# Sampled tokens' attention as a pipeline over batches, and keys and values with stationary weights, in a decoder step on one NeuronCore

## Chip, cores and metric

The kernel is one program on one core of a Trainium2 chip. The metric is its device time in microseconds (us). All matrix work runs on TensorE (PE), element work on VectorE (DVE), ScalarE (ACT) and GpSimd (POOL); SyncE (SP) and POOL issue the DMAs.

## What is computed

One step of a two-layer decoder for 256 prompt tokens and 8 batches of 8 sampled tokens (320 columns together). Layer 0 is a feed-forward block, a convolution module and another feed-forward block; its result gives the keys and values that layer 1 attends to. Cut to what the change touches:

```python
rows = (rmsnorm(x, g_kv) @ w_kv).reshape(B, T, 6, N_KV, HEAD_DIM)   # k_cmp v_cmp k_slc v_slc k_win v_win
kc = compress(k_cmp rows); vc = compress(v_cmp rows)                # gelu(blocks @ w1 + b) @ w2 + b2
p_c = masked_softmax(q kc * scale - slope * dist)                   # compressed branch
imp = (p_c summed over the group) @ overlap                         # importance of 33 blocks of 64 rows
idx = top_k(score(imp), 16)                                         # selected branch reads these blocks
o = g0 * attend(kc, vc) + g1 * attend(selected blocks) + g2 * attend(window of 512)
```

For a sampled batch the keys are 2048 paged rows in 16 pages (selected branch, all rows scored and the blocks not chosen pushed to -1e30), 512 window rows, 127 compressed rows and the 8 new rows.

## The kernel before

**Activations** are kept transposed, channels on partitions and 320 tokens on the free axis. A float32 product is three products of fp32r halves (`product`, L562 to L564). Weights stream in slabs of 1 MB: SP loads one, ACT splits off the high half (`split`, L1045), DVE the low half (`low`, L1406), PE multiplies it. `ffn`, `slabs` and `down` are loops over slabs.

**Keys and values** (phase `kv`, 6 slabs of 256 columns, one for each kind of row). `kv` in the PE program makes the tokens the stationary operand and streams the 256 columns of weights: for each of 3 token tiles (128, 128, 64) and 8 k-steps one `product`, 72 matmuls for a slab. DVE's `kv_rows` (L1701, L1703) scales them into `rows` and `rowsS`. Then 12 transposes (L791) turn the rows of the selected and the window keys into `kT`, and ACT copies them (L1259).

**The prompt's compression** comes after the query phase `q` and the gates. POOL has written the rows to `out_kv_prompt`; SP reads them back in blocks of 16 rows (L448) with the first layer's weights (L449). The class `Compression` then works 16 steps: ACT relays a piece (L1131), PE turns it (L673), ACT copies it out (L1137), PE multiplies it (`first_layer`, L813), and in the end the second layer. The prompt's attention starts behind it (L826).

**The cached compression** (8 batches) uses the same class inside layer 0, with gathers on POOL (L504) for half a batch at a time.

**Attention of the sampled tokens.** In a loop over the batches PE's `batch_scores` works in this order: transposes of the last batch's probabilities (`turn_probs`, L922) mixed with the transposes of this batch's keys (`turn_keys`, L943, 10 groups of 4), the compressed scores, the importance (L968, L974), five chunks of 512 scores (`chunk`, L937), and then `batch_values` of the batch before (L986, 92 small products). DVE adds the bias to each chunk (L1878), picks the blocks, finds the window's maximum (L1902), adds the drop to 2048 columns (L1907), finds the maximum of 2112 (L1909); ACT takes the exponentials (L1358, L1361); DVE scales by the sums (L1916, L1917); only then can the probabilities be turned. There is one score area `S`. Pages of keys go to `kpg`, issued by SP, pages of values to `vpg`, issued by POOL (`load_pages`, L329 to L331: a register load, an address and a DMA for each page); SP also loads each batch's window rows (1 MB, L464) into one of two slots of `W`. The engines are in order: what waits on an engine holds up all behind it.

Of the kernel before, what the change touches and what calls it, by code (L numbers as in the profile page):

```python
# [14 lines left out]
P = 128  # L15
# [42 lines left out]
S_SEL, S_NEW, S_WIN, S_WNEW, S_CMP = 0, PAST, PAST + TS, PAST + TS + WIN, PAST + 2 * TS + WIN  # L58
S_COLS = S_CMP + P
CREDIT = 2  # L60


def host_constants():
# [39 lines left out]
        ("sel_bias", sel_bias), ("cmp_bias_p", cmp_bias_p.reshape(P, -1)),  # L103
    ]
# [55 lines left out]
def program(nc, ins, outs, where):  # L160
    with ExitStack() as ctx:
# [43 lines left out]
        cslot = sb("cslot", P, CS, dt=I32)  # L205
# [23 lines left out]
        def slab_views(*shape):  # L229
# [29 lines left out]
        RTp = area(HF, 0, 2, 2, 66)  # L259
# [6 lines left out]
        STGp = [area(GF, u * 4096, 8, 512) for u in range(2)]  # L266
        qT = area(GF, 8192, KT, T)
        w1p = area(GF, 8192 + KT * T, 2, 16, P)
        PT = area(GF, 8192 + KT * T, 23 * P)
        qbd = area(GF, 8192 + KT * T + 23 * P, 2, P)  # L270
        selb = area(HF, 0, PAST)
        KTb = area(SF, 0, 2, PAST)
        S = area(SF, 4096, S_COLS)
        KTw = area(SF, 4096 + S_COLS, 2, WIN)
        osb = tmp[:, 0, 0:P]
        ips = tmp[:, 1, 0:P]
        wst = [W[:, u, :].rearrange("p (r c) -> p r c", r=WR) for u in range(2)]
# [20 lines left out]
            conv_step ln_step hist_out cen_ready idx_ready slot_ready rt_turned rt_ready rl_ready vnew_ready  # L298
            z_ready gelu_ready kv_ready kv_out conv_turned conv_rows stored kT_turned kT_out prow_loaded
# [3 lines left out]
            s_scores s_biased c_max c_exp c_scaled imp_sum imp_sumout imp_ready s_max s_exp s_scaled pt_turned  # L303
            pt_out o_ready o_copied o_turned o_out qbd_ready selb_loaded ptrow_loaded y_turned y_out pool_step""".split()
# [4 lines left out]
        gathered = [sem("gathered0"), sem("gathered1")]  # L309
        half_used = [sem("half_used0"), sem("half_used1")]  # L310
        K_loaded, V_loaded, K_used, V_used = map(sem, ("K_loaded", "V_loaded", "K_used", "V_used"))
        V_last_loaded = sem("V_last_loaded")
        win_loaded = [sem("win_loaded0"), sem("win_loaded1")]
        win_used = [sem("win_used0"), sem("win_used1")]
# [4 lines left out]
        OUTS_KV = 2 * (FT + KT) + KT + 4 + 6  # L319
        OUTS_DOWN10 = OUTS_KV + FT + KT  # L320

        cache = ins["cache_kv"]

        def load_pages(eng, b, c, page, used, count, loaded):

            eng.wait_ge(used, count)
            eng.sem_inc(m["passed"], 1)
            for k in range(NPAGE):
                n = eng.value_load(ptrow[0:1, bass.ds(b * NPAGE + k, 1)], min_val=0, max_val=NPOOL - 1)  # L329
                src = cache[bass.ds(n, 1), :, c, :, :].rearrange("a t g d -> t (a g d)")  # L330
                eng.dma_start(page[:, k, :], src).then_inc(loaded, 16)  # L331


        def sp_program(sp):
# [96 lines left out]
            slabs("kv", wide(ins["w_kv"].rearrange("(k p) n -> p k n", p=P)))  # L431
# [12 lines left out]
            sp.wait_ge(m["kv_stored"], 16)  # L444
            sp.wait_ge(m["evac_done"], OUTS_DOWN10 + CREDIT)
            for u in range(2):
                src = outs[2][0].rearrange("(n s) c g d -> n s (c g d)", s=CS)[:, 8 * u:8 * u + 8, 0:512]
                sp.dma_start(STGp[u][0:NCP], src).then_inc(m["prow_loaded"], 16)  # L448
                sp.dma_start(w1p[:, u, :, :], ins["w_cmp1"][u].rearrange("(j s) d h -> (s d) j h", s=2)) \  # L449
                  .then_inc(m["w1p_loaded"], 16)  # L450
# [17 lines left out]
            with sp.Fori(0, NB // 2 - 1) as i:  # L468
                for u in range(2):
                    load_keys(i, u + 1)  # L470
# [17 lines left out]
        def pool_program(pool):  # L488
# [54 lines left out]
            with pool.Fori(1, NB - 1) as b:  # L543
                load_pages(pool, b, 3, vpg, V_used, b + 1, V_loaded)
# [1457 lines left out]
```

## Time and profile before

| | |
|---|---|
| median of 3 runs | 1906.74 us (1906.7 to 1912.01) |
| the profiled execution: time, span | 1903.35 us, 1901.5 us |
| busy: PE, DVE, ACT, POOL | 1729.9, 1178.8, 720.4, 217.7 us |
| chain that ended last | PE 83%, DVE 8%, ACT 3%, issue 3% |
| mean granted clock of TensorE | 0.934 |

The profiled execution spent 1.85 us outside its span. A busy PE counts matmuls whose ends are modelled, so intervals between starts are the better measure. PEclk is the granted clock of TensorE: 1.00 is 2.4 GHz, 0.50 is 1.2 GHz. An "idle before" is put down to the releaser that came last.

### The profile page before, as it was taken

What the parts mean: (1) busy time and instruction counts of PE and PEld (TensorE: products, weight loads), DVE (VectorE), ACT (ScalarE), POOL (GpSimd) and SP (SyncE); (2) the same over time, 40 slices, a digit from 0 to 9 for tenths busy, and PEclk for the clock granted to TensorE, in tenths of its full rate; (3) what the DMA queues carried; (4) which work ended last, traced back from release to release, by engine and by line L of the source; (5) the groups of instructions that cost most, each with busy time, mean ns of one, the idle gap of its engine ahead of it and who ended that gap; (6) DMA issues with size and microseconds to landing.
All of it is one profiled execution on the core that took longest, in us unless ns stands there. A gap on an engine that the chain in (4) does not pass through costs nothing.

```text
span 1901.5 us, 35340 instructions
## 1 busy us (share of the span) xinstructions
PE 1729.9 (91%) x12409; PEld 1599.1 (84%) x12409; DVE 1178.8 (62%) x2082; ACT 720.4 (38%) x1090; POOL 217.7 (11%) x294
## 2 busy tenths in 40 slices
PE   6999999999999699999999999988857666999996
PEld 5999998788787699999999999976635545899995
DVE  6665565788886776655456655315566665766644
ACT  4332343555555443333233333235323424333321
POOL 0000021344453000000010000011003321000000
PEclk9999999899999899999999999957878888999998
DMA  5556575344445545545455545631035556455452
GB/s 145 155 152 170 146 203 148 105 116 124 120 126 209 172 124 142 153 137 155 128 159 148 154 129 156 128 97 41 7 117 191 180 176 183 125 155 144 130 152 66
DMA packets 368061, 264.72 MB, mean 139 GB/s; under 512 B 30880, under 2 KB 350867, under 8 KB 366689
## 3 DMA queue, kind: packets, MB, share of 16 engines
q1 hardware_dynamic: 350640, 202.77, 38.5%
q0 software_dynamic: 17344, 60.89, 10.2%
q8 instruction: 53, 0.87, 0.2%
q14 instruction: 24, 0.19, 0.0%
HBM read 259.95 MB, written 12.64 MB: 143 GB/s over the span
## 4 chain that ended last, share of the span: by engine, by line
PE 83%; DVE 8%; ACT 3%; issue 3%; SPq 1%; DMA 1%; DVEq 0%; POOL 0%; ACTq 0%
PE PSA L562 23%; PE PSA L564 22%; PE PSA L563 22%; PE PSA L673 3%; PE PSA L943 2%; PE PSA L937 2%; PE PSA L922 1%; PE PSA L870 1%; DVE small L1909 1%; PE PSA L813 1%; DVE S_f L1907 1%; DVE S_f32r L1406 1%; PE PSA L704 1%; PE PSA L703 1%; DVE S_f L1878 1%
## 5 line engine op out<-in xcount | busy, mean ns | idle before, releaser
L562 PE MATMUL PSA<-H_f32r,S_f32r 128*128 128x320 f32 (+1 forms) x1984 | 656.8, 331 | 25.3 <-DVE H_f32r L1542 24.3
L564 PE MATMUL PSA<-H_f32r,S_f32r 128*128 128x320 f32 (+1 forms) x1984 | 642.3, 324 | 0.0
L563 PE MATMUL PSA<-H_f32r,S_f32r 128*128 128x320 f32 x1728 | 539.9, 312 | 0.0
L1406 DVE TENSOR_TENSOR S_f32r<-W,S_f32r 128x2048 fp32r<-128x2048 f32 (+1 forms) x178 | 365.0, 2051 | 120.3 <-ACT S_f32r L1045 112.7
L562 PEld LDWEIGHTS PSA<-H_f32r,S_f32r 128*128 128x128 f32 x1984 | 379.3, 191 | 36.4 <-issue 23.5
L1045 ACT ACTIVATE S_f32r<-W 128x2048 fp32r<-128x2048 f32 (+1 forms) x178 | 305.2, 1714 | 272.7 <-PE PSA L564 260.3
L564 PEld LDWEIGHTS PSA<-H_f32r,S_f32r 128*128 128x128 f32 x1984 | 378.8, 191 | 11.9
L563 PEld LDWEIGHTS PSA<-H_f32r,S_f32r 128*128 128x128 f32 x1728 | 329.8, 191 | 0.5 <-issue 0.2
L563 PE MATMUL PSA<-G_f32r,S_f32r 128*128 128x320 f32 (+1 forms) x960 | 320.2, 334 | 0.0
L562 PE MATMUL PSA<-G_f32r,S_f32r 128*128 128x320 f32 x704 | 217.7, 309 | 1.2 <-DVE S_f32r L1406 1.2
L564 PE MATMUL PSA<-G_f32r,S_f32r 128*128 128x320 f32 x704 | 217.6, 309 | 0.0
L1078 ACT ACTIVATE tmp<-tmp 128x320 f32<-128x320 f32 x96 | 45.4, 472 | 443.5 <-DVE tmp L1476 443.5
L563 PEld LDWEIGHTS PSA<-G_f32r,S_f32r 128*128 128x128 f32 x960 | 182.0, 190 | 5.9
L1476 DVE TENSOR_TENSOR tmp<-PSA,stat 128x320 f32<-128x320 f32 x96 | 47.2, 491 | 181.9 <-PE PSA L564 181.0
L1649 DVE SCALAR_TENSOR_TENSOR H_f<-G_f,wdw,H_f 128x256 f32<-128x256 f32 x480 | 152.3, 378 | 0.0
L504 POOL DMA_INDIRECT G_f<-in_cache_kv,cslot x128 | 128.2, 1002 | 48.9 <-issue 35.8
L562 PEld LDWEIGHTS PSA<-G_f32r,S_f32r 128*128 128x128 f32 x704 | 132.2, 188 | 1.4 <-issue 1.4
L564 PEld LDWEIGHTS PSA<-G_f32r,S_f32r 128*128 128x128 f32 x704 | 132.2, 188 | 0.0
L331 POOL DMA_DIRECT2D G_f<-in_cache_kv x112 | 62.4, 557 | 504.8 <-issue 504.8
L1137 ACT ACTIVATE H_f32r<-PSA 128x512 fp32r<-128x512 f32 x128 | 76.7, 599 | 114.0 <-PE PSA L673 113.4
L1639 DVE TENSOR_TENSOR G_f32r<-PSA,H_f32r 128x512 fp32r<-128x512 f32 x128 | 88.3, 690 | 47.4 <-ACT H_f32r L1137 47.4
L673 PEld LDWEIGHTS PSA<-const,W 128*128 128x128 f32 (+1 forms) x576 | 73.9, 153 | 25.8 <-issue 4.7
(259 smaller groups left out, 1890.7 us busy)
## 6 DMA issues: line engine op xcount, KB each, us to landing
W<-in_w_ff_in SPq DMA_DIRECT2D x176, 512.0 KB, 5.0
W<-in_w_ff_out SPq DMA_DIRECT2D x64, 704.0 KB, 4.5
G_f<-in_cache_kv SPq DMA_DIRECT2D x144, 128.0 KB, 2.4
G_f<-in_cache_kv POOLq DMA_DIRECT2D x112, 128.0 KB, 3.0
W<-in_w_pw SPq DMA_DIRECT2D x16, 512.0 KB, 5.1
W<-in_state_kv_win SPq DMA_DIRECT2D x8, 1024.0 KB, 6.7
out_win_sample<-in_state_kv_win POOLq DMA_DIRECT2D x1, 8064.0 KB, 9.7
W<-in_w_kv SPq DMA_DIRECT2D x6, 1024.0 KB, 5.0
```

The lines of the kernel that those rows point to most:

```text
L331: eng.dma_start(page[:, k, :], src).then_inc(loaded, 16)
L504: pool.indirect_dma_start(out=STG[u][:, s, :], out_offset=None, in_=pairs, in_offset=bass.IndirectOffsetOnAxis(ap=cslot[:, 8 * u + s:8 * u ...
L562: pe.matmul(out, w[0], x[0], start=start, stop=False)
L563: pe.matmul(out, w[0], x[1], start=False, stop=False)
L564: return pe.matmul(out, w[1], x[0], start=False, stop=stop)
L673: tr = pe.transpose(PS[5 + c][:, g * n:g * n + n], RL[0:n, c, g * P:g * P + P], ident[0:n, 0:n])
L1045: act.activation(flat_slab[u][HI][:, 0:ph.cols], flat_slab[u][RAW][:, 0:ph.cols], ACT.Copy) \
L1137: act.activation(self.RT[:, j % 2, c, 0:4 * n], PS[5 + c][:, 0:4 * n], ACT.Copy) \
L1406: dve.tensor_tensor(lo, raw, hi, ALU.subtract).then_inc(m["lo_ready"], 1)
L1476: dve.tensor_tensor(tmp[:, u, :], PS[2 * u + gate][:, 0:T], stat[:, 2, :], ALU.mult) \
L1639: dve.tensor_tensor(RTs[1][:, j % 2, c, 0:4 * P], PS[5 + c][:, 0:4 * P], RTs[0][:, j % 2, c, 0:4 * P], ALU.subtract).then_inc(m["rt_ready" ...
L1649: dve.scalar_tensor_tensor(o, x(b * TAPS_AT_ONCE + (a + 1)), wdw[:, bass.ds(b * (TAPS_AT_ONCE * KT) + (a * KT + KT + k), 1)], o, ALU.mult, ...
```

## The change

Three things change at once.

1. **Keys and values.** The weights become the stationary operand: `keys_and_values` does 8 k-steps by 2 halves of one `product` with 320 columns, 48 matmuls for a slab, and leaves keys and values transposed. `turn_rows` turns each of the 6 results into rows (6 transposes), in the middle of the next slab. For the first two kinds DVE copies the transposed rows into `blocksT` (8 copies each), and the prompt's first and second layer of the compression run right behind the last slab and between the first two slabs of `up10`. Its relays, transposes and the way through DRAM are gone.
2. **Attention of the sampled tokens.** Two score areas take turns. `chunk` adds the drop itself, by two more matmuls of 512 columns (`dropT` by `block_keys`) on the four chunks of the selected branch; DVE adds bias and finds the minimum of the negated scores in one instruction (`tensor_tensor_reduce`); the sums and gates are applied to the output (`combine`), not to the probabilities. The keys of the next batch are turned between the chunks of this one, and the values of the batch before come behind the chunks. Pages are loaded in quads with their own semaphores. The window rows move from SP's queue to POOL's and have three slots.
3. **Cached compression.** The gathers are released and awaited by pairs; the loop is written out, and the copy of the indices is gone.

```diff
+        def load_quad(eng, b, i, c, page, loaded):
+            _, numbers = nc.values_load_multi_w_load_instructions(
+                ptrow[0:1, b * NPAGE + QUAD * i:b * NPAGE + QUAD * i + QUAD], engines=[eng.engine], ...
+            for k, n in enumerate(numbers, QUAD * i):
+                eng.dma_start(page[:, k, :], src).then_inc(loaded[i], 16)
...
+                if c == 1:
+                    sp.wait_ge(m["evac_done"], OUTS_DOWN01 + CREDIT)
+                    for w in range(2):
+                        sp.dma_start(w1p[:, w, :, :], ins["w_cmp1"][w]...).then_inc(m["w1p_loaded"], 16)
...
-            with pool.Fori(1, NB - 1) as b:
-                load_pages(pool, b, 3, vpg, V_used, b + 1, V_loaded)
+            load_window(1)
+            for b in range(1, NB):
+                if b > 2:
+                    pool.wait_ge(win_used, b - 2)
+                    load_window(b)
+                for i in range(QUADS):
+                    if b < NB - 1:
+                        pool.wait_ge(V_used, QUADS * (b - 1) + i + 1)
+                        load_quad(pool, b, i, 3, vpg, V_loaded)
...
+            def turn_rows(c):
+                pe.wait_ge(m["evac_done"], OUTS_DOWN01 + CREDIT + c + 1)
+                for t, (at, n) in enumerate(TOK_TILES):
+                    for h in range(2):
+                        mm = pe.transpose(out, src[:, h, at:at + n], ident)
+            def keys_and_values(first):
+                for c in range(ph.n):
+                    for k in range(KT):
+                        if c and k == KT // 2:
+                            turn_rows(c - 1)
+                        for h in range(2):
+                            mm = product(PS[2 * u + h][:, 0:T], [W256[u][p][:, k, h * P:h * P + P] for p in (HI, LO)],
+                                         [x[:, k, :] for x in hR], k == 0, k == KT - 1)
...
+            keys_and_values(rows_in(row_mean))
+            prompt_first_layer(0)
+            prompt_first_layer(1)
+            turn_rows(PH["kv"].n - 1)
+            ffn("10", mean=False, between=prompt_second_layer)
...
-            prompt.batch(NB)
-            prompt.end(NB)
...
+            def chunk(b, c):
+                for q in range(2):
+                    mm = pe.matmul(bank[half, :], qbd[:, u, q, half], keys, start=True, stop=c == QUADS)
+                if c < QUADS:
+                    pe.wait_ge(m["drop_out"], b + 1)
+                    for q in range(2):
+                        mm = pe.matmul(bank[half, :], dropT[blocks, half], block_keys[blocks, :], start=False, stop=True)
...
+            def values(b):
+                value(AT_WIN, 21, TS, rowsS[:, 5, :], first=True)
+                for c in range(WR):
+                    mm = value(AT_WIN, NPAGE + c, P, wst[b][:, c, 256:512], last=c == WR - 1)
+                mm.then_inc(win_used, 1)
+                value(AT_CMP, 22, P, vc[:, b, :], first=True, last=True)
+                value(AT_SEL, 20, TS, rowsS[:, 3, :], first=True)
+                for k in range(NPAGE):
+                    mm = value(AT_SEL, k, P, page[:, k, :], last=k == NPAGE - 1)
+                    if k > QUAD and k % QUAD == 1:
+                        mm.then_inc(V_used, 1)
+            def turn_out(b):
+                pe.wait_ge(m["o_combined"], b + 1)
+                pe.matmul(PS[7][0:HD, 256:384], osb, ident, start=True, stop=True).then_inc(V_used, 1)
...
+            for b in range(NB):
+                chunk(b, 0)
+                chunk(b, 1)
+                small_scores(b + 1); turn_quad(b + 1, 0)
+                chunk(b, 2)
+                turn_quad(b + 1, 1)
+                chunk(b, 3)
+                importance_sum(b + 1)
+                chunk(b, 4)
+                importance(b + 1)
+                values(b - 1)
+                turn_quad(b + 1, 2)
+                turn_probs(b, 0); turn_probs(b, 1)
+                turn_out(b - 1)
+                turn_quad(b + 1, 3)
+                turn_probs(b, 2); turn_probs(b, 3)
+                turn_drop(b + 1); turn_quad(b + 1, 4)
+                turn_probs(b, 4); turn_probs(b, 5)
```

(In the last piece the conditions `if more` and `if b` are left out, and some calls share a line.)

The order on POOL, in the loop over the batches of the sampled tokens: one register load, then an address and a DMA for a page. Before, for each page:

```order
L329 ISA [waits V_used]
L329 TENSOR_LOAD ptrow
L329 ISA x2
L331 ISA
L331 DMA G_f<-in_cache_kv 128x256
L329 ISA
L329 TENSOR_LOAD ptrow
L329 ISA x2
L331 ISA
L331 DMA G_f<-in_cache_kv 128x256
```

Now, at the last quad of batch 2's values and the window rows of batch 3 (L349 is the page's DMA, L546 the window's):

```order
L344 TENSOR_LOAD ptrow [waits V_used]
L349 ISA
L349 DMA G_f<-in_cache_kv 128x256
L349 ISA
L349 DMA G_f<-in_cache_kv 128x256
L349 ISA
L349 DMA G_f<-in_cache_kv 128x256
L349 ISA
L349 DMA G_f<-in_cache_kv 128x256
L546 DMA W<-in_state_kv_win 128x2048 [waits win_used]
L344 TENSOR_LOAD ptrow [waits V_used]
```

The register load stands once for four pages, and the window's DMA stands behind the last quad of the batch before.

The order on PE from the turned output to the window keys, one batch's turn (L1093, L1094 `turn_out`; L1005 keys; L1062 probabilities; L1026 the drop):

```order
L1093 MATMUL PSA<-const,tmp 64x128 [waits o_combined]
L1094 MATMUL PSA<-const,tmp 64x128
L1005 MATMUL PSA<-const,G_f 128x128 [waits kt_out0,K_loaded3]
L1005 MATMUL PSA<-const,G_f 128x128 x3
L1005 MATMUL PSA<-const,G_f 128x128 [waits kt_out1]
L1005 MATMUL PSA<-const,G_f 128x128 x3
L1062 MATMUL PSA<-const,S_f 128x128 [waits pt_out,s_exp]
L1062 MATMUL PSA<-const,S_f 128x128 x3
L1062 MATMUL PSA<-const,S_f 128x128 [waits pt_out,s_exp]
L1062 MATMUL PSA<-const,S_f 128x128 x3
L1026 MATMUL PSA<-const,G_f 128x128 [waits drop_ready]
L1005 MATMUL PSA<-const,W 128x128 [waits kt_out1,win_loaded0]
```

Seventeen transposes stand between the output's turn, which frees the last quad of value pages, and the first use of the next batch's window rows.

## Rows read from the trace of the kernel before

**Rows 1.** The page's chain that ended last, by engine

```profile
PE 83%; DVE 8%; ACT 3%; issue 3%; SPq 1%; DMA 1%; DVEq 0%; POOL 0%; ACTq 0%
```

**Rows 2.** Windows: length, busy of PE, PEld, DVE, ACT, POOL; PEclk, DMA share, GB/s

```profile
1235.00:1266.00 31.00, 28.98 (x150) 24.46 (x150) 0.70 (x3) 14.40 (x39) 0.00 (x0) 0.50 0.04 10
1365.80:1607.10 241.30, 162.72 (x2272) 114.49 (x2272) 149.21 (x335) 82.93 (x164) 53.72 (x96) 0.85 0.53 162
```

**Rows 3.** Timeline of DVE (start, length): two `kv` slabs, then two of `up10`

```profile
911.34 0.88 DVE L1701 TENSOR_SCALAR rows<-PSA,rtok 128x256 f32 x2 [1.79 <-PE PSA L564]
919.84 0.88 DVE L1701 TENSOR_SCALAR rows<-PSA,rtok 128x256 f32 x2 [4.38 <-PE PSA L564]
...
969.42 0.49 DVE L1476 TENSOR_TENSOR tmp<-PSA,stat 128x320 f32<-128x320 f32 x1 [5.33 <-PE PSA L564]
...
976.46 0.49 DVE L1476 TENSOR_TENSOR tmp<-PSA,stat 128x320 f32<-128x320 f32 x1 [1.91 <-PE PSA L564]
```

**Rows 4.** Timeline of PE between `kv` and `up10`

```profile
953.34 0.28 PE L564 MATMUL PSA<-S_f32r,H_f32r 128*64 128x256 f32 x1
954.97 0.44 PE L791 MATMUL PSA<-const,rows 128*128 128x128 f32 x2 [1.35 <-DVE rowsS L1703]
...
959.42 0.61 PE L562 MATMUL PSA<-H_f32r,S_f32r 128*128 128x320 f32 x1 [2.10 <-DVE H_f32r L1542]
```

**Rows 5.** Chain that ended last (start, length): the prompt's compression and what follows

```profile
1239.24 1.04 PE PSA L813 x4
...
1266.06 7.04 PE PSA L826 x64
```

**Rows 6.** Timeline of DVE: the sampled tokens' gates

```profile
1236.49 0.35 DVE L1726 TENSOR_REDUCE gateS<-tmp 128x24 f32<-128x192 f32 x1
```

**Rows 7.** Timeline of PE in the sampled tokens' attention

```profile
1412.22 1.96 PE L986 MATMUL PSA<-G_f 128*32 128x64 f32 x126
...
1431.63 1.18 PE L943 MATMUL PSA<-const,W 128*128 128x128 f32 x8 [0.26 <-ACT S_f L1340]
1432.65 0.39 PE L968 MATMUL PSA<-const,S_f 128*128 128x128 f32 x2
...
1437.91 1.94 PE L937 MATMUL PSA<-S_f,G_f 128*64 128x512 f32 x8 [0.98 <-DVE S_f L1878]
...
1454.35 1.91 PE L943 MATMUL PSA<-const,G_f 128*128 128x128 f32 x8
```

**Rows 8.** Timeline of DVE in one batch of it

```profile
1439.89 0.69 DVE L1878 TENSOR_TENSOR S_f<-PSA,const 128x512 f32<-128x512 f32 x1 [0.17 <-PE PSA L937]
...
1441.29 2.28 DVE L1907 TENSOR_TENSOR S_f<-S_f,imp 128x2048 f32<-128x2048 f32 x1
1443.60 2.35 DVE L1909 TENSOR_REDUCE small<-S_f 128x1 f32<-128x2112 f32 x1
```

**Rows 9.** Timeline of PE: the stage's first and last instructions

```profile
1365.85 0.69 PE L937 MATMUL PSA<-kT,G_f 128*64 128x64 f32 x8 [2.40 <-DVE G_f L1833]
...
1375.92 1.08 PE L937 MATMUL PSA<-S_f,G_f 128*64 128x512 f32 x4 [0.61 <-issue]
...
1604.62 0.30 PE L1005 MATMUL PSA<-const,tmp 128*128 128x128 f32 x1 [0.46 <-ACT tmp L1366]
```

**Rows 10.** Lines L329 and L331 (ns min/median/max) and one issue of POOL's timeline

```profile
L329 POOLq TENSOR_LOAD <-ptrow x112: 284/295/488, 1266.1 to 1585.6; - x112
...
L331 POOLq FUSED_REGOPS  x112: 46/46/51, 1267.3 to 1586.1; - x112
...
1437.61 0.54 POOL L331 DMA_DIRECT2D G_f<-in_cache_kv  x1 [0.69 <-issue]
```

**Rows 11.** DMA issues: engine, count, KB each, median us from issue to landing

```profile
W<-in_state_kv_win SPq DMA_DIRECT2D x8, 1024.0 KB, 6.7
...
out_kv_prompt<-rows POOLq DMA_DIRECT2D x1, 1024.0 KB, 4.6
...
G_f<-in_w_cmp SPq DMA_DIRECT2D x2, 0.5 KB, 10.6
```

More of the change, by code:

```diff
@@ L320, in program @@
         OUTS_DOWN10 = OUTS_KV + FT + KT
+        KV_TEMP = (0, 1, 3, 5)
         cache = ins["cache_kv"]
[L324 to L329, printed above, removed]
+        def load_quad(eng, b, i, c, page, loaded):
+            _, numbers = nc.values_load_multi_w_load_instructions(
+                ptrow[0:1, b * NPAGE + QUAD * i:b * NPAGE + QUAD * i + QUAD], engines=[eng.engine], min_val=0,
+                max_val=NPOOL - 1, skip_runtime_bounds_check_because="a page table holds numbers of pages of the pool")
+            for k, n in enumerate(numbers, QUAD * i):
@@ L980, in batch_values, with small_scores @@
-            def batch_values(i, off, page=vpg, loaded=None):
-                b, u = i * 2 + off, off % 2
-                def value(c, n, v, first=False, last=False):
+            def small_scores(b):
+                u = b % 2
+                pe.wait_ge(m["qbd_ready"], b + 1)
+                if b:
+                    pe.wait_ge(m["drop_out"], b)
+                for at, n, keys in ((0, TS, lambda q: kT[:, 0, q, SEQ:]), (TS, TS, lambda q: kT[:, 1, q, SEQ:]),
+                                    (2 * TS, P, lambda q: kcT[:, b, q, :])):
+                    for q in range(2):
+                        half = slice(q * HD, q * HD + HD)
+                        mm = pe.matmul(PS[4][half, at:at + n], qbd[:, u, q, half], keys(q), start=True, stop=True)
+                mm.then_inc(m["sm_scores"], 1)
@@ L1018, in pe_program @@
+            values(NB - 1)
+            turn_out(NB - 1)
             pe.wait_ge(m["o_out"], 2 * NB)
@@ L1108, in down, with ffn @@
                     seen.add(m["h_raw"], KT)
-            def ffn(name, after, mean=True):
+            def ffn(name, after, mean=True, before=None):
                 if mean:
                     root()
-                glu("up" + name, "down" + name, ACT.Silu)
+                glu("up" + name, "down" + name, ACT.Silu, before)
                 down("down" + name, after)
@@ new lines, in dve_program @@
+            scaled_cmp(0)
+            keys(0, 5)
+            select(0)
+            for r in range(6, TURNS):
+                keys(0, r)
+            queries_of(1)
+            for b in range(NB):
+                more = b + 1 < NB
+                chunk(b, 0)
+                chunk(b, 1)
+                if more:
+                    small_biased(b + 1)
+                chunk(b, 2)
+                if more:
+                    scaled_cmp(b + 1)
+                chunk(b, 3)
+                chunk(b, 4)
+                if more:
+                    select(b + 1)
+                if b:
+                    combine(b - 1)
+                if more:
+                    keys(b + 1, 5)
+                weights(b)
+                if b:
+                    out(b - 1)
+                if b + 2 < NB:
+                    queries_of(b + 2)
+                if more:
+                    for r in range(6, TURNS):
+                        keys(b + 1, r)
```

745 lines of the change are left out of this document (410 added, 335 removed).

## The prediction

> **What bounds the kernel now.** I read the page's chain first: PE holds 83% of it [rows 1]. Most of that is the slabs of weights, which the change leaves alone. Then windows of the two places where something is left to win. In the prompt's compression (31.0 us) PE counts as busy for 28.98 us, but at a granted clock of 0.50, the lower level, and the stage does only small transposes and products [rows 2]. In the sampled tokens' attention (241.3 us) PE is busy for 162.7 us and DVE for 149.2 us, neither full [rows 2]: here the chain changes hands. DVE's timeline shows why. After the last chunk come 2.28 us for the drop and 2.35 us for the maximum [rows 8], then the exponential, then scaling, and PE turns nothing until they are done. From the first chunk of batch 0 (1375.92) to the end (1604.92) 8 batches take 229 us, 28.6 us each [rows 9].
>
> **Keys and values.** Before, DVE's evacuations of two slabs lie 8.50 us apart; two slabs of 48 products with 320 columns lie 7.04 us apart [rows 3]. Six slabs: 6 x (7.04 - 8.50) = -8.8 us. Five `turn_rows` inside them are 30 transposes; 8 transposes at the higher clock took 1.02 us [rows 7], so 0.12 us each with their share of the gaps: +3.5 us. DVE is idle for 4.38 us before an evacuation now [rows 3], 2.9 us when a slab takes 7.04; its 8 small copies on each of the first two slabs (an estimated 2 us) and ACT's two copies out fit in, so I count them at nothing. Without that cover they would cost some 2 us on each of these two slabs.
>
> Behind the last slab the old kernel has 15.8 us from 953.62 to about 969.4, where the first slab of `up10` is done [rows 3, 4]: 12 transposes, two idle stretches (1.35 and 2.10 us), and then a slab that took 10.0 us where 7.04 is the rule [rows 3, 4]; I put the 3 us down to the lower clock behind the pauses. The new kernel first does 32 products of 64 columns, two records each. Four records took 1.04 us at the lower clock [rows 5]; at the higher one I take half, 0.13 us a record, which no row shows. The same products ran at a granted clock of 0.50 in the old stage [rows 2], and here they follow dense work at 1.00; I take a third of their time at the higher level and the rest at the lower: 12.4 us. Six transposes at the lower clock (8 took some 1.7 us, [rows 7]) are 1.2 us, and the slab again 9.7 us: 23.3 us, that is +7.5 us. The bounds are 8.3 + 0.7 + 7.0 = 16 us (+0.2) and 16.6 + 1.2 + 10.0 = 27.8 us (+12). The second layer, 20 records, goes between two slabs: +2.4 us. Fewer small means: -0.7 us. Sum: **+4 us**, from -3 to +8. The first layer's weights (1 MB twice) now stand on SP's queue ahead of the third slab. Such a pair needed 10.6 us to land in company [rows 11], and the slab is wanted about as long after its issue; so it may come up to 3 us late. I take nothing and keep the 3 us for the range.
>
> **The prompt's compression.** Its stage goes. Before, the gates were done on DVE at 1236.84 [rows 6], and the scores of the prompt (L826) began at 1266.06 [rows 5]. Now they begin as soon as the gates are out: **-29 us**. Late next would be the prompt's bias table, issued when the gates' products are done, but it is read only behind the 7.04 us of L826 [rows 5]. I take from -27 to -29.
>
> **The sampled tokens' attention.** PE's work for one full batch at the higher clock: nine pairs of 512-column matmuls. Two chunks of one pair took 1.94 us [rows 7], so 0.97 us each; the four drop pairs have 32 rows in place of 128, which no row shows. I take the same, 0.97 us, since as many columns stream. If the halves did not run side by side it would be twice that; less than half, no. 9 x 0.97 = 8.7 us. Keys and probabilities: 64 transposes in groups, 7.6 us [rows 7]. Values: 126 records in 1.96 us [rows 7], so 184 in 3.0 us. The rest (small scores, importance, output): 1.7 us. Together **21 us**, and DVE has no more to do than before: it loses 2.28 + 2.35 us and scaling. Its new fused instruction lies between the 0.69 us of the plain addition [rows 8] and about twice that; even then DVE stays below PE.
>
> But one wait takes the place of the removed ones, on **POOL's queue**. The quads of batch b's value pages are released from within `values(b-1)`, and the window rows of batch b+1 are issued behind the last of these quads; yet PE wants them in the same turn, 17 transposes after `turn_out`. POOL needs 0.54 us for a DMA [rows 10] plus some 0.08 us of register work (the address's part is 0.046 us [rows 10]), 0.62 us, and 0.3 us for the load of four numbers [rows 10]: 2.8 us a quad, 11.2 us for four. Before it was 1.23 us a page (0.54 and 0.69 idle). Then the 1 MB must land: 4.6 us for one such DMA from POOL, 6.7 us for the window from SP in company [rows 11]; I take 5.0.
>
> Counted from the moment R at which the window rows are in: 3.2 us for the 15 transposes left at the lower clock (PE has stood still for some 10 us, and after such a pause 8 transposes took 1.7 us and not 1.0, [rows 7]); chunks, keys, small scores and importance to the start of `values` 13.3 us, counted with about 3 us more for the lower clock's rest; 1.7 us until the first quad of values is read: R + 18.2. POOL: + 11.2. Landing: + 5.0. So this turn takes **34.4 us** and not 21, and not the 28.6 of before. It hits batches 3 to 7, five turns.
>
> The sum: up to the first chunk 11 us (10.1 before, [rows 9]; picking batch 0's blocks is now ahead of it); turn 0 without values 19.5; turn 1 21.0; turn 2 up to its R 13.3 + 11.2 + 5.0 = 29.5; four more at 34.4, 137.6; the rest of turn 6 3.2; turn 7 and the last values and output 24.6 (with the first slab of `o` split in parallel). 246.4 us, against 1604.9 - 1365.85 = 239.1 before [rows 9]: **+7 us**. With POOL's bare 0.54 us for a page, 4.6 us of landing and the clock never low the turn would be 28.5 and the stage -22; with 39 us a turn +30.
>
> A rule of the Trainium skill speaks otherwise. "DMA: Bandwidth & Descriptors", section "Issuing engines are not separate DMA queues", says that the issuing engine only matters for the sequencer's time, usually small beside the transfer. By that the window would be in time and the stage 61 us shorter; here the row has 0.54 us of issue for each 128 KB page, so sixteen are not small. The same page's section "Anatomy of one DMA" fits 2.0 us plus bytes over 436 GB/s, an estimate of 4.4 us for 1 MB, near the row's 4.6; the sum would be 3 us less.
>
> The cached compression is bound by PE, whose order there is unchanged, and POOL issues as many gathers as before, released earlier; part 3 is nothing, and the gathers' slack is what hides it.
>
> **Sum:** +4 - 29 + 7 = -18 us on the profiled span: 1883.5 us, with the 1.85 us around it 1885.4. The median of the runs is 3.4 us above the profiled one: **1889 us**.
>
> **Rivals.**
> *The window is in time.* Either POOL issues much faster or the last turn's DMAs are otherwise early. Then the turns are 21 us: 11 + 19.5 + 6 x 21 + 21.6 = 178, -61 us, in all -86: 1821 us. For it: nothing but the rule above. Against it: the rows, and an order that leaves PE 17 transposes, about 2.2 us, for 7.4 us at the least (one quad and 4.6 us of landing). By my count even that quad starts late. Chance 0.10.
> *POOL as slow as before.* If a page still costs POOL 1.23 us [rows 10], through the register work or an address computed for each page, four quads take 19.7 us in place of 11.2, and five turns get 8.5 us longer: +42, in all +24, **1931 us, slower than before**. The result turns to slower from 0.88 us a page on (18 us over five turns are 3.6 us for 16 pages). For it: 0.69 us of idle stand before each DMA now. Against: the register load, 0.295 us, now stands once in four, and the checks are gone from the order. Chance 0.12, with the nearby case of drop pairs at twice the price.
> *The narrow work behind the keys brings the clock down further,* so that 27.8 us and 3 us for a late third slab come: +8 more, 1897 us. Still faster. Chance 0.13. What is left, 0.65, is the forecast, part of it with turns of 30 to 33 us, 1865 to 1882.
>
> **Range.** A measurement of this kernel tells 0.3%, 5.7 us, from no change. From 1840 (half of the gain of a window that is little late) to 1908: 8 in 10. Faster 0.78, same 0.09, slower 0.13.
>
> **What would show it.** In the new profile: `kv` evacuations 7.6 us apart; L826's counterpart some 1 us after the gates, PEclk 0.50 still; two records of the drop for each key matmul, of 0.5 us; in turns 2 to 6 an idle PE of about 10 us before the first transpose of window keys, released by a DMA into `W` or `rows`, and POOL's DMAs 0.62 us apart in that time, the 1 MB behind them. Period 34 us there, 21 in turn 1. If PE never waits for a window, or the period is 21 to 25 us throughout, this is wrong; so too if the wait is for V pages, for `s_exp`, or for the drop.

## Result, and the profile after

| | before | changed |
|---|---|---|
| median, 20 runs each | 1911.18 us (1903.11 to 1918.62) | 1902.89 us (1897.78 to 1909.14) |
| profiled execution: time, span | 1903.35, 1901.5 us | 1900.80, 1899.0 us |
| busy: PE, DVE, ACT, POOL | 1729.9, 1178.8, 720.4, 217.7 us | 1728.7, 1127.0, 709.3, 224.5 us |
| mean granted clock | 0.934 | 0.942 |

The ratio is 0.9962, 95% interval 0.9948 to 0.9975: faster by 0.4%, some 7 us, where I had forecast 18 us. One execution of the last version below (experiment 10) took 7976 us, for a reason that no run shows, and stands outside its ratio. Busy times tell nothing: DVE lost 52 us of work and the kernel 7. The page's chain by engine has a new entry beside [rows 1]:

```profile
PE 84%; DVE 5%; issue 3%; DMA 3%; ACT 3%; SPq 1%; POOLq 1%; POOL 0%; DVEq 0%; ACTq 0%
```

DVE went from 8% to 5%, and DMA from 1% to 3%: DVE's part in the chain became smaller and a DMA's larger. The stages stand in series, so I cut the span at events that both programs have.

| stretch | before | changed | difference | forecast |
|---|---|---|---|---|
| start to the gates | 1236.49 | 1235.16 | -1.3 | +4 |
| gates to the prompt's scores | 29.57 | 0.45 | -29.1 | -29 |
| the prompt's scores to the sampled tokens' | 99.79 | 105.13 | +5.3 | 0 |
| sampled tokens' attention, to the first slab of `o` | 241.30 | 262.57 | +21.3 | +7 |
| `o` to the end | 294.35 | 295.69 | +1.3 | 0 |

Windows of the third and fourth stretch, changed kernel (columns as in [rows 2]):

```profile
1235.61:1340.74 105.13, 80.55 (x510) 66.80 (x511) 51.16 (x94) 44.92 (x166) 8.18 (x7) 0.73 0.10 33
1340.74:1603.31 262.57, 187.90 (x2433) 109.94 (x2433) 95.33 (x343) 80.92 (x165) 54.12 (x101) 0.87 0.47 146
```

In the attention DVE's work fell from 149 to 95 us [rows 2] and the stage grew by 21 us. PE is busy for 188 of 263 us. PE's timeline, at the transposes of each batch's window keys, says where the rest is (L1005 out of `W` or `rows`; in brackets the idle time ahead and its releaser):

```profile
1367.96 1.09 PE L1005 MATMUL PSA<-const,rows 128*128 128x128 f32 x8
1391.21 1.16 PE L1005 MATMUL PSA<-const,W 128*128 128x128 f32 x8 [0.27 <-DVE S_f L2060]
1426.59 1.97 PE L1005 MATMUL PSA<-const,W 128*128 128x128 f32 x8 [12.36 <-DMA W<-in_state_kv_win]
1463.04 1.97 PE L1005 MATMUL PSA<-const,rows 128*128 128x128 f32 x8 [10.24 <-DMA rows<-in_state_kv_win]
1500.18 1.97 PE L1005 MATMUL PSA<-const,W 128*128 128x128 f32 x8 [13.22 <-DMA W<-in_state_kv_win]
1537.76 1.97 PE L1005 MATMUL PSA<-const,W 128*128 128x128 f32 x8 [13.72 <-DMA W<-in_state_kv_win]
1575.52 1.97 PE L1005 MATMUL PSA<-const,rows 128*128 128x128 f32 x8 [13.94 <-DMA rows<-in_state_kv_win]
```

Five turns wait 10 to 14 us for a window, and then start at the lower clock (1.97 us for eight transposes, 1.1 us where there was no pause). The four distances are 36.5, 37.1, 37.6 and 37.8 us; turn 1, whose window was there, took 23.3 us. POOL's timeline of one such turn, quads of V pages (L349) and then the window (L546):

```profile
1446.70 2.32 POOL L349 DMA_DIRECT2D G_f<-in_cache_kv  x4 [26.75 <-PE PSA L1070]
1449.43 2.32 POOL L349 DMA_DIRECT2D G_f<-in_cache_kv  x4 [0.41 <-issue]
...
1454.90 2.32 POOL L349 DMA_DIRECT2D G_f<-in_cache_kv  x4 [0.42 <-issue]
1457.21 0.53 POOL L546 DMA_DIRECT2D rows<-in_state_kv_win  x1
```

A quad takes 2.73 us (2.8 forecast, from 0.54 us a page in [rows 10]). In the chain of waits stand the register load with which POOL goes on when PE has released the first quad, and the window's landing:

```profile
1445.73 0.33 POOLq L344
...
1457.21 5.79 DMA rows<-in_state_kv_win
```

So the window's DMA is issued 11.5 us behind that release and lands 5.8 us later.

The keys and values, DVE's evacuations in the changed kernel (in the place of the first two of [rows 3]), with the first of `up10` behind them:

```profile
908.88 0.79 DVE L1863 TENSOR_TENSOR G_f<-PSA,stat 128x640 f32<-128x640 f32 x1
...
918.79 0.82 DVE L1863 TENSOR_TENSOR G_f<-PSA,stat 128x640 f32<-128x640 f32 x1
...
928.46 0.83 DVE L1863 TENSOR_TENSOR kT<-PSA,stat 128x640 f32<-128x640 f32 x1 [4.27 <-PE PSA L590]
...
936.14 0.82 DVE L1863 TENSOR_TENSOR G_f<-PSA,stat 128x640 f32<-128x640 f32 x1 [3.39 <-PE PSA L590]
...
951.53 0.82 DVE L1863 TENSOR_TENSOR G_f<-PSA,stat 128x640 f32<-128x640 f32 x1 [3.39 <-PE PSA L590]
...
966.32 0.49 DVE L1633 TENSOR_TENSOR tmp<-PSA,stat 128x320 f32<-128x320 f32 x1 [4.35 <-PE PSA L590]
```

The last three distances are 7.7 us as forecast (7.6), but the first two 9.9 and 9.7 us, with an idle PE of 2.83 us ahead of the third slab. And from the last slab to the first of `up10` it is 14.8 us, where I had 23.3 and a lower bound of 16. PE's timeline in that seam:

```profile
951.33 7.25 PE L685 MATMUL PSA<-G_f 128*128 128x64 f32 x64
...
958.42 0.82 PE L658 MATMUL PSA<-const,G_f 128*128 128x128 f32 x6
```

The first slab of `up10` starts at 959.00. The 64 records of the first layer took 7.1 us, 0.11 us each, against 0.26 us at the lower clock [rows 5].

### The profile page after: what moved, and what is told of

It reads as the page before. It is cut to its first block, busy times and chain, and to the rows that moved or that the text cites. A ratio compares the mean times of both kernels' runs of the same rounds, so it can differ in the third digit from the quotient of the medians.

```text
span 1899.0 us, 33769 instructions
## 1 busy us (share of the span) xinstructions
PE 1728.7 (91%) x12379; PEld 1572.6 (83%) x12379; DVE 1127.0 (59%) x2094; ACT 709.3 (37%) x1065; POOL 224.5 (12%) x285
## 3 DMA queue, kind: packets, MB, share of 16 engines
q1 hardware_dynamic: 349344, 194.12, 37.1%
q0 software_dynamic: 18496, 69.28, 11.5%
## 4 chain that ended last, share of the span: by engine, by line
PE 84%; DVE 5%; issue 3%; DMA 3%; ACT 3%; SPq 1%; POOLq 1%; POOL 0%; DVEq 0%; ACTq 0%
PE PSA L588 22%; PE PSA L590 22%; PE PSA L589 22%; PE PSA L743 3%; PE PSA L1039 2%; PE PSA L1045 2%; PE PSA L1005 2%; PE PSA L929 1%; DMA W<-in_state_kv_win 1%; PE PSA L1070 1%; DVE S_f32r L1558 1%; PE PSA L1062 1%; PE PSA L838 1%; PE PSA L774 1%; PE PSA L773 1%
## 5 line engine op out<-in xcount | busy, mean ns | idle before, releaser
L588 PE MATMUL PSA<-H_f32r,S_f32r 128*128 128x320 f32 (+1 forms) x2080 | 686.6, 330 | 25.5 <-DVE H_f32r L1699 21.8
L590 PE MATMUL PSA<-H_f32r,S_f32r 128*128 128x320 f32 (+1 forms) x2080 | 671.4, 323 | 0.0
L589 PE MATMUL PSA<-H_f32r,S_f32r 128*128 128x320 f32 x1824 | 568.9, 312 | 0.0
L588 PEld LDWEIGHTS PSA<-H_f32r,S_f32r 128*128 128x128 f32 x2080 | 396.7, 191 | 37.0 <-issue 20.8
L590 PEld LDWEIGHTS PSA<-H_f32r,S_f32r 128*128 128x128 f32 x2080 | 396.4, 191 | 11.9
L589 PEld LDWEIGHTS PSA<-H_f32r,S_f32r 128*128 128x128 f32 x1824 | 347.2, 190 | 0.5
L512 POOL DMA_INDIRECT G_f<-in_cache_kv,cidx x128 | 138.9, 1085 | 432.7 <-DVE cidx L1748 266.6
L743 PEld LDWEIGHTS PSA<-const,W 128*128 128x128 f32 x512 | 66.1, 146 | 22.2 <-issue 3.1
L743 PE MATMUL PSA<-const,W 128*128 128x128 f32 x512 | 80.0, 280 | 4.8 <-ACT W L1256 2.6
```

The costliest lines, as they stand in the source:

```text
L512: pool.indirect_dma_start(out=STG[s // 8][:, s % 8, :], out_offset=None, in_=pairs, in_offset=bass.IndirectOffsetOnAxis(ap=cidx[:, b * CS ...
L588: pe.matmul(out, w[0], x[0], start=start, stop=False)
L589: pe.matmul(out, w[0], x[1], start=False, stop=False)
L590: return pe.matmul(out, w[1], x[0], start=False, stop=stop)
L743: tr = pe.transpose(PS[5 + c][:, g * n:g * n + n], RL[0:n, c, g * P:g * P + P], ident[0:n, 0:n])
```

## Experiments

My theory after the result: the forecast named the right mechanism (the window stands behind four quads of V pages on POOL), and its sum failed on sizes. The rivals: the window is late for its bytes and not for its place; PE's idle time swallows whatever is saved; the DMA engines are the limit. Ratios are to the kernel before in the same session; 1% is 19 us.

**1. The window ahead of the quads.**

```diff
-                if b > 2:
-                    pool.wait_ge(win_used, b - 2)
-                    load_window(b)
+                if 1 < b < NB - 1:
+                    pool.wait_ge(win_used, b - 1)
+                    load_window(b + 1)
```

> The changed kernel, with batch b+1's window rows issued on POOL's queue ahead of batch b's quads of V pages, not behind them; their slot was freed a turn earlier. Theory (the window is late because it stands behind four quads whose last is released at the turn's end): the idle PE of about 12 us before the first transpose of window keys in turns 2 to 6 goes, each of these turns falls from the 37.2 us measured to about 23.3 us as turn 1 has it, and the lower clock behind the pauses with it; 5 turns x 14 us = 70 us, about 1833 us. Rival A (the DMA engines are the next limit: 5 MB for each batch in 23 us would be 228 GB/s, where the whole stage ran at 144): turns of 27 to 30 us with waits for pages of K or V in the window's place, 1850 to 1865 us. Rival B (the window load is late for its own landing, not for its place in the queue): turns stay above 33 us, over 1880 us.

Measured: 1836.44 us, ratio 0.9612 (0.9582 to 0.9643), 3.5% or 67 us below the changed kernel's 0.9962. The attention fell from 262.6 to 196.2 us. Its windows, and PE's timeline at window keys:

```profile
1347.42:1543.62 196.20, 180.22 (x2433) 104.39 (x2433) 94.62 (x343) 80.63 (x165) 54.12 (x101) 0.97 0.63 196
```

```profile
1420.20 1.16 PE L1005 MATMUL PSA<-const,W 128*128 128x128 f32 x8 [0.18 <-DVE S_f L2060]
1443.52 1.16 PE L1005 MATMUL PSA<-const,rows 128*128 128x128 f32 x8 [0.21 <-DVE S_f L2060]
1465.83 1.16 PE L1005 MATMUL PSA<-const,W 128*128 128x128 f32 x8 [0.19 <-DVE S_f L2060]
...
1528.34 1.29 PE L1070 MATMUL PSA<-G_f 128*32 128x64 f32 x39 [5.02 <-issue]
1529.92 1.08 PE L1070 MATMUL PSA<-G_f 128*32 128x64 f32 x32 [0.28 <-DMA G_f<-in_cache_kv]
```

In the first three rows no window is waited for; the turns take 22.1 to 23.3 us, the granted clock is 0.97. The mean rate, 196 GB/s, is the stage's own pace. The wait of 5.02 us is not one for V pages: it stands behind record 57 of 128, and PE waits for a quad only ahead of records 1, 33, 65 and 97 (the last section has what it was). Rival A shows itself only at the very end, in the chain's landing of batch 6's last V page:

```profile
1517.84 12.04 DMA G_f<-in_cache_kv
```

PE wanted this page for its last 32 records, and without the pause of 5 us it would, by my estimate from these starts, have stood for it nearly as long.

**2. The window on SP's queue again.** POOL issues V pages alone; in SP's loop, behind the second quad of K pages of the same batch:

```diff
                     load_quad(sp, b, i, 2, kpg, K_loaded)
+                    if b > 2 and i == 1:
+                        sp.wait_ge(win_used, b - 2)
+                        sp.dma_start(W_slots[wslot[b]], src).then_inc(win_later[wslot[b]], 16)
```

> The changed kernel, with the window rows of batches 3 to 7 back on SP's queue, as they were before the change: behind the second quad of the same batch's K pages, a turn ahead of their use (their own three semaphores). POOL issues V pages alone. Theory (the window was late for the four quads ahead of it, on whatever queue): PE never waits for a window, turns of about 22.7 us as with the early window on POOL, about 1837 us. Rival (the queue matters: SP already issues 16 K pages a turn, and one more DMA of 1 MB there makes K pages late): turns of 25 us or more with waits for K pages, over 1850 us.

Measured: 1837.09 us, ratio 0.9625 (0.9595 to 0.9654), turns of 22.0 to 23.1 us, no wait for a window or a K page (2.0 us for a V page in the last turn). So it is the place in the order and not the queue that counts.

**3. Twice the issues.**

```diff
-                eng.dma_start(page[:, k, :], src).then_inc(loaded[i], 16)
+                for h in range(parts):
+                    rows_ = slice(h * P // parts, (h + 1) * P // parts)
+                    eng.dma_start(page[rows_, k, :], src[rows_]).then_inc(loaded[i], 16)
```

> The changed kernel, with each V page of the sampled tokens loaded by two DMAs of 64 KB on POOL's queue and not one of 128 KB: twice the issues ahead of the window's DMA, the same bytes. Theory (POOL's time for 16 issues lies in series in each late turn): the stretch from the first release of a quad to the window's issue goes from 11.8 us to about 21 us (16 more issues of 0.58 us), turns 2 to 6 from 37.2 to about 46.5 us, the whole +46 us, about 1949 us. Rival (the late window is a matter of bytes and landing, POOL's issues lie beside it): below +10 us.

Measured: 1950.45 us, ratio 1.0212 (1.0176 to 1.0247), 48 us above the changed kernel. PE at two windows:

```profile
1440.94 1.97 PE L1007 MATMUL PSA<-const,W 128*128 128x128 f32 x8 [20.83 <-DMA W<-in_state_kv_win]
1487.99 1.97 PE L1007 MATMUL PSA<-const,rows 128*128 128x128 f32 x8 [21.91 <-DMA rows<-in_state_kv_win]
```

The turns take 45.8 us on average (the last of these rows stands at 1624.24), 8.6 us more for 16 issues more (9.3 expected). By links, on average over four turns: from the window's arrival to the release of the first quad 18.2 us (18.4 in the changed kernel), from there to the window's DMA 22.3 us (12.6), landing 5.3 us (6.2). The issues lie in series with everything. By the rule of the Trainium skill that the prediction cites ("DMA: Bandwidth & Descriptors", "Issuing engines are not separate DMA queues": issuing is usually small beside the transfer) this edit would have cost next to nothing; here it cost 48 us.

**4. Less work for a PE that waits.** The two matmuls of the drop are left out (`for q in range(0)`).

> The changed kernel without the products of the drop in the sampled tokens' scores: no block is pushed down, all 2048 rows count (this part of the computation is left out). It takes away 16 records of 0.25 us in each turn, 4.0 us. Theory (PE's own work from the window's arrival to the first release of a V quad, 19.2 us, is in series with POOL's issues and the landing): turns 2 to 6 shorten by 4 us each in spite of PE being idle for 12 us of them, and so do turns 0, 1 and 7: -32 us, about 1871 us. Rival (PE is idle for a third of such a turn, so work taken from it only lengthens the idle time): only turns 0, 1 and 7 gain, -12 us, about 1891 us.

Measured: 1867.15 us, ratio 0.9778 (0.9742 to 0.9813), 35 us below the changed kernel:

```profile
1477.39 1.97 PE L1005 MATMUL PSA<-const,W 128*128 128x128 f32 x8 [11.60 <-DMA W<-in_state_kv_win]
1509.94 1.97 PE L1005 MATMUL PSA<-const,W 128*128 128x128 f32 x8 [11.68 <-DMA W<-in_state_kv_win]
```

Late turns are 32.4 us on average and not 37.2: PE waits nearly as long as before, and what it no longer does (4.0 us) comes off the turn in full. In the first three of these turns the first quad is released 13.8 to 14.9 us behind the window's arrival, where it was 18.4 us on average with the drop. A stage can have its bottleneck engine idle for a third of the time and still be shortened by taking work from it, when that work lies between the arrival of one buffer and the release of the next.

**5. The same with the window early.**

> The changed kernel with the window rows issued early and without the products of the drop (no block is pushed down, that part of the computation is left out). With the window early a turn took 22.7 us. Theory (PE bounds the turns then): 4 us less in each of 8 turns, 18.7 us a turn, -32 us against the early window with its drop, about 1804 us. Rival (the DMA engines are nearly the limit: 5.2 MB a turn is 230 GB/s at 22.7 us and would be 280 GB/s at 18.7 us; the last turn with the early window already waited 5 us for V pages): turns of 20 to 22 us with waits for pages, 1812 to 1830 us.

Measured: 1808.41 us, ratio 0.9465 (0.9428 to 0.9503), 28 us below experiment 1: between the two. PE's timeline:

```profile
1370.10 1.09 PE L1005 MATMUL PSA<-const,rows 128*128 128x128 f32 x8
...
1387.68 1.16 PE L1005 MATMUL PSA<-const,W 128*128 128x128 f32 x8 [0.18 <-DVE S_f L2060]
...
1403.81 0.65 PE L1070 MATMUL PSA<-G_f 128*32 128x64 f32 x30 [3.29 <-issue]
...
1410.54 1.16 PE L1005 MATMUL PSA<-const,W 128*128 128x128 f32 x8 [0.19 <-DVE S_f L2060]
1428.19 1.16 PE L1005 MATMUL PSA<-const,rows 128*128 128x128 f32 x8 [0.19 <-DVE S_f L2060]
```

The turns from batch 1 on take 17.6, 22.9, 17.6, 18.3, 22.1 and 17.6 us. In the two long ones PE stands for 3.3 and 2.5 us among the value products and goes on at the lower clock. This is no wait for V pages: the last quad of the first of them was issued from 1391.3 to 1393.1 us and took at most 5.4 us to land, and PE stood until 1403.81 (again, see the last section). PE waits for V pages in the last turn alone, 3.6 and 2.7 us. The mean rate of the stage is 226 GB/s. So the rival's waits for pages in every turn did not come, and nothing here shows that the DMA engines limit turns of 17.6 us; that kernel leaves out work, and with the drop PE bounds the turns.

**6. The compression's weights spread out.**

```diff
-                if c == 1:
+                if c in (2, 3):
                     sp.wait_ge(m["evac_done"], OUTS_DOWN01 + CREDIT)
-                    for w in range(2):
+                    for w in (c - 2,):
```

> The changed kernel, with the two loads of 1 MB of the compression's first weights behind the third and the fourth slab of keys and values on SP's queue, not both ahead of the third. Theory (the third slab is late behind them: evacuations 9.91 and 9.67 us apart where the later ones have 7.68, of which 2.8 us are an idle PE and the rest its lower clock): all five distances become 7.7 us, -4.2 us in that stage; the whole about 1899 us. Rival (the weights only move the lateness to a later slab, since a slab is asked for every 7.7 us and 1 MB takes 5 us): a later distance grows to 9 us or more and the stage gains less than 1.5 us.

Measured: 1899.85 us, ratio 0.9947 (0.9925 to 0.9968), an interval that overlaps the changed kernel's. The stage tells it better:

```profile
912.55 0.79 DVE L1863 TENSOR_TENSOR G_f<-PSA,stat 128x640 f32<-128x640 f32 x1
...
919.79 0.82 DVE L1863 TENSOR_TENSOR G_f<-PSA,stat 128x640 f32<-128x640 f32 x1 [1.87 <-PE PSA L590]
927.49 0.82 DVE L1863 TENSOR_TENSOR kT<-PSA,stat 128x640 f32<-128x640 f32 x1 [2.27 <-PE PSA L590]
...
950.57 0.82 DVE L1863 TENSOR_TENSOR G_f<-PSA,stat 128x640 f32<-128x640 f32 x1 [3.38 <-PE PSA L590]
```

First to last evacuation 38.0 us against 42.65: -4.6 us, no slab is late (the first distance has no `turn_rows` in it). The theory holds in the stage; the total cannot tell it.

**7. The first layer twice** (`for j in [*range(CS // 2)] * 2`).

> The changed kernel, with the 32 products of the prompt's first layer behind the last slab of keys and values done twice (the second time over the first, same result): 128 records of 64 columns in place of 64. I had put two thirds of them at the lower clock, 12.4 us; the changed kernel showed 7.1 us for 64 records, 0.11 us each. Theory A (narrow products as such do not bring the clock down behind dense work): +7.1 us, 14.2 us for 128 records, the slab of up10 behind them still 7.0 us. Theory B (they do, only later than after 64 records): over +10 us, the second half at 0.2 us a record or so and the slab behind it 8 to 10 us.

```profile
953.03 14.40 PE L685 MATMUL PSA<-G_f 128*128 128x64 f32 x128
967.27 0.82 PE L658 MATMUL PSA<-const,G_f 128*128 128x128 f32 x6
```

128 records in 14.24 us, 0.11 us each to the end, and the first slab of `up10` 21.94 us behind the last evacuation, 7.15 more than in the changed kernel. The total, 1912.62 us, ratio 1.0011 (0.9989 to 1.0033), is 0.5% above the changed kernel's; the 7.1 us (0.37%) lie inside the uncertainty. Theory A holds: 64 columns without a pause left the clock up.

**8. The first part alone,** in the kernel before.

> The kernel before with the first part of the change alone: keys and values with stationary weights, the rows turned behind, and the prompt's compression fed from the transposed rows; attention of the sampled tokens and cached compression as before. Theory (the stages are in series, so what the changed kernel's trace shows of this part, -1.3 us up to the gates and -29.1 us from the gates to the prompt's scores, stands alone as well): -30 us, a ratio of 0.984, about 1879 us; the attention of the sampled tokens as before, about 241 us. Then the second part has cost the changed kernel some 22 us. Rival (the parts help each other, and alone this one gives less, since pages and window rows that once loaded during the compression now come late to the old attention): under -20 us, with idle PE in batch 0.

Measured: 1880.28 us, ratio 0.9850 (0.9816 to 0.9884). Windows of the prompt's and the sampled tokens' attention:

```profile
1239.86:1340.44 100.58, 80.97 (x511) 66.66 (x511) 50.60 (x92) 44.72 (x166) 7.62 (x6) 0.72 0.13 42
1340.44:1584.01 243.57, 164.78 (x2273) 116.13 (x2273) 149.14 (x335) 83.46 (x165) 54.18 (x96) 0.84 0.52 161
```

The first part is worth 1.5%, 29 us, and the old attention takes 243.6 us (241.3 and 241.7 in two profiles of before). The changed kernel has all three parts at 0.9962, so the other two cost 0.0112 of 1907 us, 21 us, give or take 7 by the two intervals, as the stage table has it (+21.3).

**9. Is the prompt's attention slower?** Its instructions are the same, yet it took 99.8 us before and 105.1 after. I ran both kernels again, unchanged.

> The kernel before, unchanged, for a second profile. The prompt's attention, the same instructions in both kernels, took 99.8 us in the first profile of before, 105.1 in that of the changed kernel, and 99.6 to 110.1 us in the eight experiments. If that is the clock's lottery in a stage with pauses, it is 100 to 110 us here too; if the change brought it on, 99 to 101 us.

> The kernel before, unchanged, for a third profile, as for the second: 100 to 110 us for the prompt's attention if its duration is the clock's lottery, 99 to 101 us if the change lengthened it.

> The changed kernel, unchanged, for a second profile: the prompt's attention 99.6 to 110.1 us by either; the distance from one late window to the next 37.2 us as in the first.

Windows of the stage in the second profile of before:

```profile
1269.18:1377.27 108.09, 85.91 (x510) 70.98 (x511) 50.69 (x92) 46.20 (x167) 16.30 (x22) 0.67 0.18 59
```

108.1 us in the second and in the third profile of before, at a granted clock of 0.67 and not 0.76; 102.8 us in the second of the changed kernel. So no effect of the change shows; why the granted clock differs from one execution to the next stays open. The first profile of before (1903.35 us, 8 us under its kernel's later median) had a lucky stretch there. The late windows of the second profile of the changed kernel are 36.2, 36.8, 37.7 and 38.7 us apart, 37.3 on average.

**10. The better version:** experiments 1 and 6, and batch 7's V pages on SP's queue only when the same quad of batch 6 has landed.

```diff
                 sp.wait_ge(K_used, QUADS * (NB - 1) + i + 1)
+                sp.wait_ge(V_loaded[i], 16 * QUAD * (NB - 1))
```

> The changed kernel with three edits: the window rows issued early, the two loads of the compression's first weights behind the third and fourth slab of keys and values, and in the last turn the V pages of batch 7 (on SP's queue) issued only when the same quad of batch 6 has landed. Expected: the early window's 1836 us less 4.6 us (the spread, from the distances of the evacuations) less 5 to 7 us (the idle PE in the last turn, 5.0 us before a page of batch 6 and what follows at the lower clock), 1825 us. If the last turn's wait is of POOL's issues and not of the competition of SP's pages, or moves to batch 7's pages, 1831 us.

Measured: 1828.78 us, ratio 0.9573 (0.9535 to 0.9612): 4.3% below the kernel before, the fastest complete version. Against experiment 1 (0.9612) the intervals overlap; the stage shows 3.4 us from the last window's keys to `o` (29.95 us against 33.31). POOL's pages of batch 6 now land in at most 3.8 us and PE waits for none, but a pause stands in the last values:

```profile
1520.75 1.07 PE L1071 MATMUL PSA<-G_f 128*32 128x64 f32 x29 [3.69 <-issue]
```

It stands behind record 99 of 128, where PE waits for no page either.

## Why the prediction was off

The direction, the stage and the mechanism were right; the gain was forecast more than twice too large. With the clock's luck taken out (the third stretch), the terms are -1.3 - 29.1 + 21.3 + 1.3 = -7.8 us, which is what the medians show (-8.3). Luck had a part in it: the seam behind the keys and values came out 8.5 us better than forecast, and without that the kernel would have been no faster than before.

**The attention, +7 forecast, +21.3.** This is the step that failed, by the sizes of its terms: the late turn, priced at 34.4 us, takes 37.2, turn 1 takes 23.3 us and not 21.0, and turn 2 up to R 33.5 and not 29.5. To the end of the last output's turn it is 260.8 us, where the sum had 246.4:

| piece | forecast | measured |
|---|---|---|
| to the first chunk | 11 | 10.1 |
| turn 0 | 19.5 | 18.9 |
| turn 1 | 21.0 | 23.3 |
| turn 2 to R | 29.5 | 33.5 |
| four late turns | 4 x 34.4 | 4 x 37.2 |
| rest | 27.8 | 26.1 |

The late turn's three links, on average over four, with the release taken where POOL's register load starts in the chain: R to the release of the first quad 18.4 us (18.2), POOL 12.6 us (11.2), landing 6.2 us (5.0). (The expectations of experiments 3 and 4 took the release 0.3 us ahead of the first page's DMA, and so had 19.2 and 11.8.) POOL's regular time is 11.5 us, since the first DMA comes 0.97 us behind the release where I had 0.3; in the next three turns it was 11.9, 12.9 and 14.1 us, with stops between the pages that the profile puts down to issue and whose cause is open. I had taken the landing near the 4.6 us of a lone DMA, though a row beside it had 6.7 us for a window in company [rows 11]; this window lands behind 16 pages just issued. The "28.5 with everything at its bare value" was never near. In turn 2 I also left out the 1.7 us up to the first quad read, which the later turns had (2.1 measured). Turn 1 shows that a full turn is 23 us of PE and not 21: a chunk's pair is 1.005 us and not 0.97 (9.1 us for nine), the values take 4.4 us in place of 3.0, with a gap of about 1 us inside, and the rest, with the drop's transpose and the wait behind it, 2.3 us in place of 1.7; the 64 transposes took the 7.6 us forecast. That PE's link came out right in the late turns is luck: from the first chunk to `values` its work takes 12.5 us at the higher clock where I had about 10.3, and the rest of the lower clock cost 0.1 to 1.2 us where I had put 3. Small errors of a cyclic term count as often as it comes: 2.8 us times four.

**Keys and values, +4 forecast, -1.3.** Two errors against each other. The seam was 14.8 us and not 23.3: I let the clock fall because the same products had run at 0.50 in the old stage. There PE waited between them for ACT's copies; here they come without a pause (experiment 7). The first layer took 7.1 us and not 12.4, and the slab behind it 7.2, not 9.7. My lower bound of 16 was too high as well. The other way, the two weight loads, taken as 0 with 3 us kept for the range, cost 4.2 us in the first two distances (experiment 6 gives 4.6): 2.8 us of idle PE and the lower clock behind it. The spacing itself (7.7 for 7.6) and the second layer (2.1 for 2.4 us) were right.

**The prompt's compression, -29:** -29.1. **The drop:** as many records as the keys' (four for a chunk, 0.25 us each), and not half as many of 0.5 us; 1.00 us a pair where I took 0.97. **DVE out of the way:** right, no turn waits for a maximum, and for the drop 0.8 us once, at the start. But DVE was not all that held the old attention up; by its waits PE also stood 20.8 us in all for V pages, which the prediction does not mention:

```profile
PE PSA L986 <- DMA G_f<-in_cache_kv: 20.8, 6, 6.6
```

**Cached compression, 0:** from DVE's first evacuation (342.54 us before, 341.91 changed) to the reduction behind the stage (594.81, 594.16) 252.3 us in both kernels.

The rivals: "window in time" and "POOL as slow as before" did not happen. But experiment 1 shows that the first was one moved line away: 1836 us, where I had put 1821 for it with turns of 21 us. In the second rival the threshold of 0.88 us a page does not follow from its own numbers: 0.62 us and 3.6/16 us are 0.85 us, and 0.92 with the register load's share.

## What to carry to other kernels

When a load's slot is free a turn early, issue it then, ahead of the loads that are released late; a queue works in order, and a load placed behind late ones inherits their lateness. Where a cycle runs from a buffer's arrival over an engine's work to the release, the issue and the landing of the next, sum all links: any of them, even work on an engine that idles for a third of the turn, shortens it in full. Price a landing with the traffic that was issued just ahead of it, and do not carry a stage's clock over with its instructions: look at whether the pauses go along.

## What the hardware showed that I had not expected

- 128 records of 64 columns ran at the higher level (0.11 us each) for 14.2 us behind dense work; the same kind took 0.26 us each between waits [rows 5].
- The same instructions in the prompt's attention took 99.8, 108.1 and 108.1 us in three profiles of the same kernel, at a granted clock of 0.76 and 0.67. One profile is no baseline for a stage with many pauses. The Trainium skill ("TensorE: Matmul & The Clock Gate", "Part 1: The HAM clock gate") says that the number of matmuls at the lower clock at the start of a kernel varies from run to run of the same kernel. These profiles show the like for a stage in the middle of one.
- Within `values` PE stands for 0.7 to 1.5 us in most turns, at records where it waits for no semaphore; the profile puts this down to issue. The trace's DMA records tell what it is most likely: in all 51 such pauses in the attention's value products where two starts lie over 0.8 us apart, in 14 profiles, a 16 KB packet of the instruction queue (q8 on the page) ended 1.2 to 1.6 us before PE went on. For the 5.02 us in experiment 1 it ran from 1525.48 to 1526.90 us (PE went on at 1528.34), for the 3.29 us in experiment 5 from 1401.29 to 1402.41 (1403.81), for the 3.69 us in experiment 10 from 1517.87 to 1519.20 (1520.75). In the three waits there for a V page (experiments 2 and 5, 2.0 to 3.6 us, with a semaphore to wait for) none ended in that span. So PE seems to stand for its own instructions; no run changed their number or place to prove it, and why some packets start so late is open.
